# The first mixer's output product: eight half-size block products become seven

## Chip, cores and metric

The kernel runs on one core of one Trainium2 chip. The metric is the device time of one execution in microseconds (us). Before the change it is 1657.04 us, the median of 3 runs (1656.95 to 1657.22).

## The reference, cut to what matters

Two transformer blocks run one after the other on a sequence of 512 tokens with 1024 channels, all in float32. The first block has a mixer, a mixture of experts (top 2 of 32) and an embedding gate; the second has attention, a gated recurrence and a large MLP. What changes is the last product of the first mixer:

```
merged = sigmoid(gate_a) * (y_a @ w_up_a) + sigmoid(gate_b) * (y_b @ w_up_b)
x = x + merged @ w_out
h = rmsnorm(x, g_ffn)          # then the router and the experts read h
```

`merged` is 512 x 1024 and `w_out` is 1024 x 1024.

## The kernel before

TensorE multiplies in the reduced format float32r. To keep float32 accuracy every operand is split into a high part (a copy by ScalarE into float32r) and a low part (VectorE: value minus high), and each product is three matmul passes: high by high, high by low, low by high. `split_hi` (L1329) makes the high part of a weight chunk of 512 x 512, `split_lo` (L2246) the low part, `rest` (L2263) the low part of activations. `merged` lies in `ga_fm`, channels on partitions, in eight tiles of 128 channels by 512 tokens; its parts are `act_hi` and `act_lo`.

The output product before (L3742 to L3747 on TensorE): four chunks of `w_out`, each 512 channels in by 512 out. SyncE loads each into one of two buffers `w_stage` (`load_chunk`, L827) once the chunk two places ahead is split. `tile_passes` (L3445) multiplies one tile of 128 tokens by one chunk: 4 channel tiles x 3 passes = 12 matmuls of 128 x 128 by 512 columns. There are 4 chunks x 4 token tiles = 16 such groups, 192 matmuls. The first column half is summed in the PSUM banks `gb` and added to the rows `x` by VectorE (`add_tile`, L2598); in the second half the groups are paired by token tile (`paired_unit`, L3566), so that the row ends come early: each finished token tile is added, squared and scaled (`root` L1583, `scale_rows` L2268), transposed by TensorE (`turn_rows`, L3494) and multiplied by the router's weights. The transposes of rows 0 stand before the last group.

Ahead of it `g_upa` and `g_upb` (the two up-projections, 48 matmuls a unit) end in VectorE's gate and merge steps (L2557 and L2589, a pair for each of the eight tiles). VectorE's instructions follow a written order: merge pairs 0 to 3, `split_lo` of w_out's chunk 0, the low parts of merged tiles 0 to 3, merge pairs 4 to 7, `split_lo` of chunk 1, low parts of tiles 4 to 7, and then the additions. ScalarE (L1561 to L1575) alternates in the same way. SyncE's order is: weights of `g_upb`, the rows `x` again (L912), the four chunks of `w_out` (L913), the gain, the router's weights, and the experts' first weights into `ring[0]` to `ring[5]` (`load_half`, L931, 2 MB each). GpSimd issues nothing between the head sums of the mixer and the embedding gate. In the last MLP GpSimd issues transfers that add a block of weights in HBM to a block in SBUF (`add_block`, L1304).

Waits are on counting semaphores; an instruction whose wait is not met holds all that stand behind it on its engine. Here `w_stage`, `w_hi` and `w_lo` are 2 buffers each (L220 to L222).

Of the kernel before, what the change touches and what calls it, by code (L numbers as in the profile page):

```python
# [75 lines left out]
def two_blocks(nc, A, out):  # L76
# [37 lines left out]
    g_out = Gemm(g_upb, 2, 2, "dve")  # L114
# [30 lines left out]
    with ctx:  # L145
# [680 lines left out]
        def _(sp):  # L826
# [82 lines left out]
            load_units(g_upb, A["w_up_b"][0], 0)  # L909
# [3 lines left out]
            load_units(g_out, A["w_out"][0], 0)  # L913
            load_gain(1, A["g_ffn"][0])
# [20 lines left out]

            sp.dma_start(route_f[:, :, 0:NG], A["w_grp"][0].rearrange("(k p) n -> p k n", p=P))\
# [104 lines left out]
            for s in range(2):  # L1041
                sp.wait_ge(gates_stored[s], 16 * KT)
# [186 lines left out]


# [95 lines left out]
        def _(act):  # L1326
# [240 lines left out]
            for u in range(2):  # L1567
                split_hi(g_out.chunk0 + u, u)

                act.wait_ge(pe_tiles, 4 * (g_upa if u == 0 else g_upb).chunk1)  # L1570
                for k in range(4 * u, 4 * u + 4):
                    act.wait_ge(merged, k + 1)
# [2822 lines left out]
```

## Time and profile before

| | |
|---|---|
| median of the runs | 1657.04 us |
| the profiled execution | 1658.27 us, its span 1656.6 us |
| TensorE busy | 1642.8 us (99%), 10312 matmuls |
| VectorE, ScalarE, GpSimd busy | 1044.9, 718.4 and 123.2 us |
| granted TensorE clock | 0.999 |
| HBM traffic | 215 GB/s over the span |

The span runs from the first to the last instruction; the execution's own time also has what lies around it. A matmul's shown duration overlaps the next one's, so its price in a dense stream is the distance of starts. "us to landing" of a transfer counts from its issue.

### The profile page before, as it was taken

How to read it: one execution, taken by the hardware profiler on the slowest of the kernel's cores; microseconds unless marked ns; L12 is line 12 of the kernel's file. 1: busy time of each engine (PE TensorE's matmuls, PEld its weight loads, DVE VectorE, ACT ScalarE, POOL GpSimd, SP SyncE). 2: the span in 40 equal slices, each digit the busy share in tenths (PEclk: the TensorE clock that was granted, in tenths of full speed). 3: DMA queues.
4: the chain of work that ended last, by engine and by line, in shares of the span. 5: the costliest groups of instructions: out<-in, count | busy, mean ns of one | idle time of the engine just before them, and what ended most of it. 6: DMA issues, size and time to landing. Idle time of an engine off the chain costs nothing.

```text
span 1656.6 us, 25306 instructions
## 1 busy us (share of the span) xinstructions
PE 1642.8 (99%) x10312; PEld 1240.0 (75%) x10312; DVE 1044.9 (63%) x1373; ACT 718.4 (43%) x911; POOL 123.2 (7%) x175
## 2 busy tenths in 40 slices
PE   9999999999999999999999999999999999999998
PEld 7899998864545535554688877788888889889986
DVE  6989778453243334324578746567675577878887
ACT  6576553421101101111366533344643367757775
POOL 4000100000000000000111022210020000000000
PEclk9999999999999999999999999999999999999999
DMA  7132324888999999999551232124366527467864
GB/s 269 63 112 92 103 77 169 350 334 338 424 412 430 428 427 430 429 427 428 226 178 42 91 102 77 52 77 133 110 222 167 145 93 209 106 185 220 206 141 126
DMA packets 93697, 358.28 MB, mean 216 GB/s; under 512 B 8016, under 2 KB 8032, under 8 KB 81312
## 3 DMA queue, kind: packets, MB, share of 16 engines
q1 hardware_dynamic: 81264, 330.67, 52.0%
q0 software_dynamic: 12336, 26.23, 8.1%
q8 instruction: 71, 1.16, 0.3%
q14 instruction: 26, 0.21, 0.0%
HBM read 349.54 MB, written 7.34 MB: 215 GB/s over the span
## 4 chain that ended last, share of the span: by engine, by line
PE 96%; DVE 2%; DMA 1%; ACT 0%; issue 0%; POOL 0%; DVEq 0%; POOLq 0%; ACTq 0%
PE bank L3467 31%; PE bank L3896 13%; PE bank L4341 9%; PE bank L3630 9%; PE bank L4316 9%; PE bank L3909 7%; PE bank L3801 4%; PE bank L3842 3%; PE bank L4075 2%; PE bank L3492 2%; PE bank L3513 1%; DMA w_stage<-in_w_proj_gla 1%; PE bank L4105 1%; PE bank L4128 1%; PE bank L4175 1%
## 5 line engine op out<-in xcount | busy, mean ns | idle before, releaser
L3467 PE MATMUL bank<-act_hi,w_hi 128*128 128x512 f32 x544 | 215.5, 396 | 2.1 <-DVE gs_fm L2557 1.7
L3896 PE MATMUL bank<-ring,xgT 128*64 128x512 f32 x992 | 215.9, 592 | 0.6 <-ACT xgT L1641 0.6
L3467 PE MATMUL bank<-act_hi,w_lo 128*128 128x512 f32 x544 | 212.1, 390 | 0.0
L3467 PE MATMUL bank<-act_lo,w_hi 128*128 128x512 f32 x544 | 211.8, 389 | 0.0
L3896 PEld LDWEIGHTS bank<-ring,xgT 128*64 128x64 f32 x992 | 71.9, 137 | 140.2 <-issue 140.0
L1336 ACT ACTIVATE w_hi<-w_stage 128x2048 fp32r<-128x2048 f32 x50 | 95.9, 1919 | 138.9 <-PE bank L3467 128.7
L2249 DVE TENSOR_TENSOR w_lo<-w_stage,w_hi 128x2048 fp32r<-128x2048 f32 x50 | 115.2, 2303 | 62.9 <-ACT w_hi L1336 61.3
L4341 PE MATMUL bank<-down,part_hi 128*128 128x512 f32 x448 | 138.2, 390 | 0.1
L3467 PEld LDWEIGHTS bank<-act_hi,w_hi 128*128 128x128 f32 x544 | 102.1, 188 | 26.1 <-issue 2.8
L1671 ACT ACTIVATE y_hi_sb<-bank,slot_tables 128x512 fp32r<-128x512 f32 x32 | 22.0, 687 | 225.6 <-PE bank L3909 224.2
L3467 PEld LDWEIGHTS bank<-act_hi,w_lo 128*128 128x128 f32 x544 | 102.1, 188 | 21.8
L3467 PEld LDWEIGHTS bank<-act_lo,w_hi 128*128 128x128 f32 x544 | 102.2, 188 | 20.2
L3909 PE MATMUL bank<-ring,gatedT 128*64 128x512 f32 x512 | 113.4, 595 | 0.0
L2759 DVE TENSOR_TENSOR gated<-gated,bank 128x512 f32<-128x512 f32 x16 | 11.0, 688 | 161.3 <-PE bank L3896 161.3
L4341 PEld LDWEIGHTS bank<-down,part_hi 128*128 128x128 f32 x448 | 83.8, 188 | 18.2 <-issue 1.1
L3909 PEld LDWEIGHTS bank<-ring,gatedT 128*64 128x64 f32 x512 | 35.4, 137 | 69.5 <-issue 66.4
L4341 PE MATMUL bank<-down,part_lo 128*128 128x512 f32 x224 | 87.2, 389 | 0.0
L2731 DVE TENSOR_TENSOR x_tm<-x_tm,bank 128x512 f32<-128x512 f32 x128 | 78.6, 681 | 0.3 <-PE bank L3842 0.3
L2775 DVE SCALAR_TENSOR_TENSOR y_lo_sb<-bank,slot_tables,y_hi_sb 128x512 fp32r<-128x512 f32 x32 | 23.5, 751 | 69.9 <-ACT y_hi_sb L1671 69.6
L3630 PE MATMUL bank<-row_hi,slot_hi 128*128 128x256 f32 x224 | 63.5, 284 | 0.0
L4316 PE MATMUL bank<-act_lo,slot_hi 128*128 128x256 f32 x224 | 63.4, 283 | 0.0
L4316 PE MATMUL bank<-act_hi,slot_lo 128*128 128x256 f32 x224 | 63.4, 283 | 0.0
(600 smaller groups left out, 3782.8 us busy)
## 6 DMA issues: line engine op xcount, KB each, us to landing
ring<-in_w SPq DMA_DIRECT2D x93, 2048.0 KB, 14.5
w_stage<-in_w_in SPq DMA_DIRECT2D x39, 1024.0 KB, 5.2
w_stage<-in_w_ff SPq DMA_DIRECT2D x19, 1024.0 KB, 6.3
b_sum<-in_w_ff POOLq DMA_DIRECT2D x12, 1024.0 KB, 10.9
w_stage<-in_w_out SPq DMA_DIRECT2D x8, 1024.0 KB, 5.7
b_one<-in_w_ff SPq DMA_DIRECT2D x6, 1024.0 KB, 7.0
stage<-in_w_ff SPq DMA_DIRECT2D x5, 1024.0 KB, 5.6
x_tm<-in_x SPq DMA_DIRECT2D x8, 512.0 KB, 9.4
```

The source lines that it names most:

```text
L1336: act.activation(w_hi[s][:, 0:ktiles, :], w_stage[s][:, 0:ktiles, :], ACT.Copy)\
L2249: dve.tensor_tensor(w_lo[s][:, 0:ktiles, :], w_stage[s][:, 0:ktiles, :], w_hi[s][:, 0:ktiles, :].bitcast(F32), ALU.subtract).then_inc(w_lo ...
L2731: dve.tensor_tensor(xt, xt, bank[:, :], ALU.add).then_inc(moe_added, 1)
L3467: ins = pe.matmul(banks[j][:, :], left, right, start=(kc == 0 and k == 0 and n_pass == 0), stop=(kc == g.chunks - 1 and k == g.ktiles - 1 ...
L3492: return pe.transpose(dst, src, ident[0:rows, 0:rows])
L3630: ins = pe.matmul(bank_of[:, 256 * f:256 * f + 256], left[:, k, cols], right[:, k, :], start=(n in (0, 1, 3) and f == 0 and k == 0 and n_p ...
L3801: return pe.matmul(bank[:, (k % 2) * 2 * P:(k % 2 + 1) * 2 * P], part[:, t, k * P:(k + 1) * P], sel[:, t, :], start=start, stop=(part is x ...
L3842: ins = pe.matmul(bank[:, :], selT[:, t * P:(t + 1) * P], part[:, half], start=(part is y_hi_sb), stop=(part is y_lo_sb))
L3896: ins = pe.matmul(dst[mine, :], xgT[:, 4 * kh + k, slots], up_weights(2 * w + kh, q, k, ahead), start=(kh == 0 and k == 0), stop=(kh == 1 ...
L3909: return pe.matmul(gb[1 + nh][mine, :], gatedT[:, k, mine], ring[4 + k // 2][:, 4 * q + 2 * (k % 2) + nh, :], start=(k == 0), stop=(k == 3 ...
L4316: ins = pe.matmul(bank[:, 256 * f:256 * f + 256], left[:, k, cols], right[:, k, :], start=(n in (0, 1, 3) and f == 0 and k == 0 and n_pass ...
L4341: ins = pe.matmul(part_bank[h][n][j][:, :], left[:, ka, cols], right[:, k, :], start=(part_first[n] and kc == 0 and k == 0 and n_pass == 0 ...
```

## The change

`merged` is cut into token halves (near: tokens 0 to 255, far: 256 to 511) and channel halves, and `w_out` into four blocks of 512 x 512. Seven products of 256 tokens x 512 channels x 512 columns take the place of eight; each is 2 token tiles x 12 = 24 matmuls. They need sums of blocks. The weight sums T1 to T4 are made by negated copies on ScalarE (`out_negated`) and by five accumulating transfers that GpSimd issues (`out_block_added`): `o_t2` = W12 - W22 + W21, `o_t3` = W12 - W22, `o_t1` = W22 - W21, `o_t4` = W11 - T2, where W12 is rows 0 to 511, columns 512 to 1023. The four sums of activations are VectorE instructions (`out_sum`, 128 x 1024 each) in `ga_fm` and `o_s2`. Products that share a result follow each other in the same PSUM banks: VectorE adds the bank to the one place, and TensorE then goes on summing in it for the next, so products 2, 3, 5 and 6 wait for the addition of the product they continue (`out_bank`, `out_first`). SyncE loads four blocks itself: three blocks of `w_out` directly for use or as start of a sum (W11 and W21 in `w_stage`, W22 in `o_t3`) and W12 in `o_b22`. The experts' first weights move: ring 5 and 4 ahead, 0, 3, 1 and 2 during and after the products. The semaphore counts of `gates_stored`, which is used again, are raised. The core of the diff:

```diff
-    g_out = Gemm(g_upb, 2, 2, "dve")
+    g_out = Gemm(g_upb, 1, PARTS + 1, "dve", tiles=2 * PARTS)
...
+        o_t1 = at("o_t1", F + 0, [P, 4, 512])
+        o_b22 = at("o_b22", F + 16, [P, 4, 512])
+        o_t2, o_t3, o_t4 = (at(f"o_t{n}", F + page, [P, 4, 512]) for n, page in ((2, 4), (3, 20), (4, 12)))
+        o_s2 = at("o_s2", F + 48, [P, 4, 256])
+        o_t2_hi, o_t2_lo = at("o_t2_hi", F + 8, [P, 4, 512], F32R), at("o_t2_lo", F + 4, [P, 4, 512], F32R)
+        o_t4_hi, o_t4_lo = at("o_t4_hi", F + 8, [P, 4, 512], F32R), at("o_t4_lo", F + 12, [P, 4, 512], F32R)
+        o_b22_hi, o_b22_lo = at("o_b22_hi", F + 20, [P, 4, 512], F32R), at("o_b22_lo", F + 16, [P, 4, 512], F32R)
...
+        out_bank = (mb[0:2], mb[2:4], mb[2:4], mb[2:4], gb[2:4], mb[2:4], gb[2:4])
+        out_first = (True, True, False, False, True, False, False)
...
+        OUT_PLACES = ((2, 0), (2, 0), (2, 1), (0, 1), (0, 1), (0, 0), (2, 1))
+        O_SUM_2, O_SUM_4, O_SUM_3, O_SUM_1 = 32, 48, 16, 32
+        OUT_ADDS = (3, 2)
+        OH_LESS_12, OH_LESS_12_AGAIN, OH_LESS_11, OH_T2, OH_LESS_T2, OH_S2, OH_S3, OH_S1, OH_S4 = range(KT + 1, KT + 10)
+        O_S1, O_S2, O_S3, O_S4 = range(KT + 1, KT + 5)
+        OL_T2, OL_S2, OL_S3, OL_S1, OL_S4 = range(KT + 1, KT + 6)
...
-            load_units(g_upb, A["w_up_b"][0], 0)
+            load_unit(g_upb, 0, A["w_up_b"][0], 0)
+            sp.wait_ge(o_gated, NH)
+            sp.dma_start(o_t3[:, :, :], out_block(1, 1)).then_inc(out_far, 16)
...
-            load_units(g_out, A["w_out"][0], 0)
-            load_gain(1, A["g_ffn"][0])
+            for i in range(2):
+                load_chunk(g_out.chunk0 + i, i, A["w_out"][0], slice(0, 512), i)
+            sp.wait_ge(merged_high, OH_LESS_12)
+            sp.dma_start(o_b22[:, :, :], out_block(0, 1)).then_inc(out_far, 16)
...
+            sp.wait_ge(out_far, 32)
...
-            sp.wait_ge(y_lo, AT_MERGED + KT)
-            for m in range(2):
-                load_half(m, 0)
-            sp.wait_ge(w_lo_done, split_count(g_out.chunk1 - 1))
+            sp.wait_ge(y_lo, 2 * NH)
+            load_half(5, 0)
+            sp.wait_ge(merged, KT)
+            load_half(4, 0)
+            sp.wait_ge(w_lo_done, split_count(out_chunk(1)))
+            for i in range(2):
...
+            sp.wait_ge(w_lo_done, split_count(out_chunk(4)))
+            sp.wait_ge(pe_tiles, out_product(2))
+            load_half(0, 0)
+            sp.wait_ge(merged_sums, O_S4)
+            load_gain(1, A["g_ffn"][0])
...
+            sp.wait_ge(merged_low, OL_S4)
+            load_half(3, 0)
+            sp.wait_ge(pe_tiles, out_product(5))
+            load_half(1, 0)
+            sp.wait_ge(pe_tiles, 4 * g_out.chunk1)
+            load_half(2, 0)
...
+            def out_block_added(dst, i, q, n):
+                pool.dma_start(dst[:, :, :], out_block(i, q), accum_op=ALU.add).then_inc(out_block_added_in[n], 16)
+            pool.wait_ge(merged_high, OH_LESS_12)
+            out_block_added(o_t2, 0, 1, 0)
+            pool.wait_ge(merged_high, OH_LESS_12_AGAIN)
+            out_block_added(o_t3, 0, 1, 1)
+            pool.wait_ge(out_block_added_in[0], O_SUM_2 - 16)
+            out_block_added(o_t2, 1, 0, 0)
+            pool.wait_ge(merged_high, OH_LESS_11)
+            pool.wait_ge(out_block_added_in[1], O_SUM_3)
+            out_block_added(o_t1, 1, 1, 1)
+            pool.wait_ge(merged_high, OH_LESS_T2)
+            out_block_added(o_t4, 0, 0, 0)
...
+            def out_negated(dst, src):
+                act.activation(dst[:, :, :], src[:, :, :], ACT.Copy, scale=-1.0).then_inc(merged_high, 1)
+            act.wait_ge(out_far, 16)
+            out_negated(o_t2, o_t3)
             split_hi(g_upb.chunk0, 0)
+            act.wait_ge(merged_high, OH_LESS_12)
+            out_negated(o_t3, o_t3)
             for h in range(NH):
...
+            act.wait_ge(w_loaded[1], ((g_out.chunk0 + 1) // 2 + 1) * 16)
+            out_negated(o_t1, w_stage[1])
+            split_hi(out_chunk(0), 0)
+            act.wait_ge(pe_tiles, 4 * g_upa.chunk1)
+            for k in range(4):
+                act.wait_ge(merged, k + 1)
+                act.activation(act_hi[:, k, :], ga_fm[:, k, :], ACT.Copy).then_inc(y_hi, 1)
+            act.wait_ge(out_block_added_in[0], O_SUM_2)
+            act.activation(o_t2_hi[:, :, :], o_t2[:, :, :], ACT.Copy).then_inc(merged_high, 1)
+            out_negated(o_t4, o_t2)
+            split_hi(out_chunk(1), 1)
+            act.wait_ge(pe_tiles, 4 * g_upb.chunk1)
+            act.wait_ge(merged, KT)
...
+            act.wait_ge(pe_tiles, out_product(0))
+            act.wait_ge(merged_sums, O_S2)
+            act.activation(act_hi[:, near_k, far_t], o_s2[:, :, :], ACT.Copy).then_inc(merged_high, 1)
+            act.wait_ge(out_block_added_in[1], O_SUM_3)
+            act.activation(w_hi[0][:, :, :], o_t3[:, :, :], ACT.Copy).then_inc(w_hi_done, 1)
+            act.wait_ge(merged_sums, O_S3)
+            act.activation(act_hi[:, far_k, near_t], ga_fm[:, far_k, near_t], ACT.Copy).then_inc(merged_high, 1)
+            act.wait_ge(pe_tiles, out_product(1))
+            act.wait_ge(out_block_added_in[1], O_SUM_1)
+            act.activation(w_hi[1][:, :, :], o_t1[:, :, :], ACT.Copy).then_inc(w_hi_done, 1)
+            act.activation(act_hi[:, far_k, far_t], ga_fm[:, near_k, near_t], ACT.Copy).then_inc(merged_high, 1)
+            act.wait_ge(pe_tiles, out_product(2))
+            act.wait_ge(out_block_added_in[0], O_SUM_4)
+            act.activation(o_t4_hi[:, :, :], o_t4[:, :, :], ACT.Copy).then_inc(w_hi_done, 1)
+            act.wait_ge(w_lo_done, split_count(out_chunk(3)))
+            act.wait_ge(out_far, 32)
+            act.activation(o_b22_hi[:, :, :], o_b22[:, :, :], ACT.Copy).then_inc(w_hi_done, 3)
...
-            act.wait_ge(w_lo_done, split_count(g_out.chunk1 - 1))
-            for t in range(NT):
-                act.wait_ge(out_dve, g_out.tile0 + 4 + t + 1)
-                if t == 3:
-                    own.settle()
-                own.did(half_square(0, t, ssq))
+            for t in (2, 3):
+                act.wait_ge(out_dve, out_added(1, t - 2))
+                own.did(half_square(first_half(t), t, ssq))
+            act.wait_ge(early_in, EARLY_IN)
+            act.activation(early_p_hi[:, :, :], early_p[:, :, :], ACT.Copy).then_inc(p_hi, 1)
+            act.activation(early_ple_hi[:, :, :], early_ple[:, :, :], ACT.Copy).then_inc(p_hi, 1)
+            act.wait_ge(pe_tiles, out_product(4))
+            act.wait_ge(merged_sums, O_S4)
+            act.activation(act_hi[:, far_k, far_t], ga_fm[:, near_k, far_t], ACT.Copy).then_inc(merged_high, 1)
+            own.settle()
+            for t in (0, 1):
+                act.wait_ge(out_dve, out_added(4, t))
+                own.did(half_square(first_half(t), t, ssq))
             own.settle()
...
+            dve.wait_ge(merged, KT)
+            out_sum(m22, m21, m22, ALU.add)
+            split_lo(out_chunk(1), 1)
+            dve.wait_ge(y_hi, AT_MERGED + KT)
+            rest(act_lo[:, far_k, far_t], m11, act_hi[:, far_k, far_t]).then_inc(y_lo, 4)
+            dve.wait_ge(merged_sums, O_S1)
+            out_sum(o_s2[:, :, :], m22, m11, ALU.subtract)
+            dve.wait_ge(merged_high, OH_LESS_T2)
+            rest(o_t2_lo[:, :, :], o_t2[:, :, :], o_t2_hi[:, :, :]).then_inc(merged_low, 1)
+            dve.wait_ge(rows_again, 16 + 16 * NT)
+            out_low(near_k, far_t, o_s2[:, :, :], OH_S2)
+            out_add(0, 0)
+            out_add(0, 1)
+            out_sum(m21, m11, m21, ALU.subtract)
+            out_add(1, 0)
+            out_weights_low(3, w_lo[0], o_t3, w_hi[0])
+            out_add(1, 1)
+            out_low(far_k, near_t, m21, OH_S3)
+            out_add(2, 0)
+            out_low(far_k, far_t, m22, OH_S1)
+            out_add(2, 1)
+            out_weights_low(4, w_lo[1], o_t1, w_hi[1])
+            out_add(3, 0)
+            out_add(3, 1)
+            out_sum(m12, m12, o_s2[:, :, :], ALU.subtract)
+            out_weights_low(5, o_t4_lo, o_t4, o_t4_hi)
+            out_add(4, 0)
+            out_add(4, 1)
+            out_weights_low(6, o_b22_lo, o_b22, o_b22_hi, parts=3)
+            out_low(far_k, far_t, m12, OH_S4)
+            out_add(5, 0)
+            out_add(5, 1)
             def add_tile(u, j, width=512):
                 xt = x[:, j, u * 512:(u + 1) * 512]
                 return dve.tensor_tensor(xt, xt, gb[j][:, :], ALU.add)
...
-            merged_half = half_split(AT_MERGED)
-            for kc in range(2):
-                for j in range(4):
-                    merged_half(kc, j)
-                    tile_passes(g_out, g_out.chunk0 + kc, g_out.tile0 + j, kc, kc, j, fm=False)
-            paired_unit(g_out, 1, {7: lambda: turn_rows(1, 0)})
+            def out_passes(n, j):
+                k0, t0 = ((0, 256), (4, 256), (0, 256), (4, 0), (4, 256), (0, 0), (4, 256))[n]
+                hi, lo = ((w_hi[0], w_lo[0]), (w_hi[1], w_lo[1]), (o_t2_hi, o_t2_lo), (w_hi[0], w_lo[0]),
+                          (w_hi[1], w_lo[1]), (o_t4_hi, o_t4_lo), (o_b22_hi, o_b22_lo))[n]
+                cols = slice(t0 + j * P, t0 + (j + 1) * P)
+                for k in range(4):
+                    for n_pass, (left, right) in enumerate(((act_hi, hi), (act_hi, lo), (act_lo, hi))):
+                        ins = pe.matmul(out_bank[n][j][:, :], left[:, k0 + k, cols], right[:, k, :],
+                                        start=(out_first[n] and k == 0 and n_pass == 0),
+                                        stop=(k == 3 and n_pass == 2), skip_group_check=True)
+                ins.then_inc(pe_tiles, 6 if (n, j) == (PARTS - 1, 1) else 2)
+            def out_operands(n):
+                if n in out_split:
+                    pe.wait_ge(w_lo_done, split_count(out_chunk(n)))
+                if n < 2:
+                    pe.wait_ge(y_lo, AT_MERGED + 4 * n + 4)
+                elif n != 5:
+                    pe.wait_ge(merged_low, {2: OL_S2, 3: OL_S3, 4: OL_S1, 6: OL_S4}[n])
+            for n in range(PARTS):
+                out_operands(n)
+                for j in range(2):
+                    if n in (2, 3, 5, 6):
+                        pe.wait_ge(out_dve, out_added({2: 1, 3: 2, 5: 3, 6: 4}[n], j))
+                    out_passes(n, j)
+                    if (n, j) == (PARTS - 1, 0):
+                        turn_rows(1, 0)
```

## Rows read from the trace of the kernel before

**Rows 1.** The page, busy time of each engine and its share of the span.

```profile
PE 1642.8 (99%) x10312; PEld 1240.0 (75%) x10312; DVE 1044.9 (63%) x1373; ACT 718.4 (43%) x911; POOL 123.2 (7%) x175
```

**Rows 2.** The chain that ended last, 281 to 347 us: start, us, what, how many.

```profile
281.75 41.03 PE bank L3467 x181
...
330.41 1.02 PE bank L3492 x8
...
346.66 7.09 PE bank L3896 x32
```

**Rows 3.** Timeline of VectorE: start, duration, operation and shape, waits in brackets.

```profile
273.14 2.29 DVE L2249 TENSOR_TENSOR w_lo<-w_stage,w_hi 128x2048 fp32r<-128x2048 f32 x1 [0.60 <-ACT w_hi L1336]
275.35 2.49 DVE L2264 TENSOR_TENSOR act_lo<-ga_fm,act_hi 128x512 fp32r<-128x512 f32 x4
277.76 0.68 DVE L2557 TENSOR_TENSOR gb_fm<-gb_fm,bank 128x512 f32<-128x512 f32 x1
...
280.41 0.68 DVE L2557 TENSOR_TENSOR gb_fm<-gb_fm,bank 128x512 f32<-128x512 f32 x1
...
317.41 1.23 DVE L2264 TENSOR_TENSOR early_p_lo<-early_p,early_p_hi 128x1024 fp32r<-128x1024 f32 x1 [2.07 <-ACT early_p_hi L1613]
```

**Rows 4.** Timeline of ScalarE, 244 to 276 us.

```profile
244.09 1.90 ACT L1336 ACTIVATE w_hi<-w_stage 128x2048 fp32r<-128x2048 f32 x1
...
271.19 1.92 ACT L1336 ACTIVATE w_hi<-w_stage 128x2048 fp32r<-128x2048 f32 x1 [8.96 <-PE bank L3467]
273.02 2.17 ACT L1573 ACTIVATE act_hi<-ga_fm 128x512 fp32r<-128x512 f32 x4
```

**Rows 5.** Timeline of SyncE's queue, 248 to 265 us: the issues.

```profile
248.34 0.37 SPq L835 DMA_DIRECT2D w_stage<-in_w_up_b  x1
248.75 2.17 SPq L912 DMA_DIRECT2D x_tm<-in_x  x4
...
255.47 0.40 SPq L835 DMA_DIRECT2D w_stage<-in_w_out  x1
...
264.72 0.39 SPq L835 DMA_DIRECT2D w_stage<-in_w_out  x1
```

**Rows 6.** Issues of 264 to 265 us, KB and us to landing.

```profile
w_stage<-in_w_out SPq DMA_DIRECT2D x1, 1024.0 KB, 5.0
```

**Rows 7.** Windows, 250 to 261 us: length, busy time by engine, PEclk, DMA share, GB/s.

```profile
250.00:261.00 11.00, 11.00 (x50) 9.06 (x50) 10.19 (x15) 3.11 (x5) 0.00 (x0) 1.00 0.97 376
```

**Rows 8.** Accumulating transfers alone: issues at 1591 and 1595 us, and their landings.

```profile
1591.12 1.28 POOL L1307 DMA_DIRECT2D w_stage<-in_w_ff  x1 [36.94 <-ACT w_stage L1966]
1594.85 1.28 POOL L1307 DMA_DIRECT2D w_stage<-in_w_ff  x1 [2.45 <-ACT w_stage L1966]
...
w_stage<-in_w_ff POOLq DMA_DIRECT2D x1, 1024.0 KB, 8.6
...
w_stage<-in_w_ff POOLq DMA_DIRECT2D x1, 1024.0 KB, 10.8
```

**Rows 9.** An accumulating and a plain transfer issued together at 1258 us, and their landings.

```profile
1258.16 1.41 POOL L1307 DMA_DIRECT2D b_sum<-in_w_ff  x1 [39.36 <-ACT b_sum L1966]
...
b_sum<-in_w_ff POOLq DMA_DIRECT2D x1, 1024.0 KB, 11.2
w_stage<-in_w_out SPq DMA_DIRECT2D x1, 1024.0 KB, 5.7
```

**Rows 10.** A plain transfer issued behind two accumulating ones, at 1527.84 us; timeline and landing.

```profile
1524.95 2.60 POOL L1307 DMA_DIRECT2D b_sum<-in_w_ff  x2 [8.70 <-DMA b_sum<-in_w_ff]
...
w_stage<-in_w_ff SPq DMA_DIRECT2D x1, 1024.0 KB, 14.8
```

**Rows 11.** Windows in the experts, 700 to 750 us; columns as in rows 7.

```profile
700.00:750.00 50.00, 50.00 (x262) 25.38 (x260) 17.42 (x40) 4.96 (x8) 0.00 (x0) 1.00 1.01 429
```

**Rows 12.** Timeline of TensorE at the kernel's start, the first matmuls after it was idle.

```profile
6.38 2.04 PE L3513 MATMUL bank<-w_hi,raw_hi 128*128 128x512 f32 x4
8.23 1.35 PE L3513 MATMUL bank<-w_lo,raw_hi 128*128 128x512 f32 x4
```

More of the change, by code:

```diff
@@ L531, in two_blocks @@
         counters, COUNTERS = att_masked, NT + 3
+        out_far, merged_sums, merged_high, merged_low = route_in, merged, x_hi, x_lo
+        out_block_added_in = gates_stored
         early_stored = (wsp_masked, ln_sd)
@@ L625, in loaded, with block_in @@
         def loaded(h, buffers, k):
-            base, per = {"one": (1, ONE_LOADS), "sum": (2, SUM_LOADS), "added": (KT, ADDS)}[buffers]
+            base, per = {"one": (1, ONE_LOADS), "sum": (2, SUM_LOADS)}[buffers]
             return 16 * (base + per * h + k)
+        def block_in(n, h, k):
+            return 16 * (OUT_ADDS[n] + KT + ADDS * h + k)
         def weight_block(h, i, q, kc):
@@ L947, in _ @@
                 .then_inc(early_in, 16)
-            for m in range(2, 6):
-                load_half(m, 0)
-            sp.wait_ge(pe_tiles, 4 * g_out.chunk1)
+            sp.wait_ge(w_lo_done, split_count(out_chunk(4)))
[3 more added lines that the diff above has]
+            load_gain(1, A["g_ffn"][0])
+            sp.wait_ge(pe_tiles, out_product(4))
             for q in range(2):
@@ L1566, in _ @@
             split_hi(g_upb.chunk0 + 1, 1)
[L1567 to L1572, printed above, removed]
-                    act.activation(act_hi[:, k, :], ga_fm[:, k, :], ACT.Copy).then_inc(y_hi, 1)
-            split_hi(g_out.chunk0 + 2, 0)
-            split_hi(g_out.chunk0 + 3, 1)
-            def half_square(u, t, sums):
-                half = slice(u * 512, (u + 1) * 512)
+            act.wait_ge(w_loaded[1], ((g_out.chunk0 + 1) // 2 + 1) * 16)
@@ L1580, in half_square @@
+            act.wait_ge(out_block_added_in[0], O_SUM_4)
[3 more added lines that the diff above has]
+            act.activation(o_b22_hi[:, :, :], o_b22[:, :, :], ACT.Copy).then_inc(w_hi_done, 3)
+            def half_square(half, t, sums):
                 return act.activation(squared[t % 3][:, :], x[:, t, half], ACT.Square, scale=float(D) ** -0.5,
@@ L1583, in root @@
             def root(t):
-                act.wait_ge(out_dve, g_out.tile0 + 4 + NT + t + 1)
-                own.did(half_square(1, t, half_ms))
+                act.wait_ge(out_dve, out_added(5, t) if t < 2 else out_added(6, t - 2))
+                own.did(half_square(second_half(t), t, half_ms))
                 own.settle()
@@ new lines, in _, with out_sum, out_low, out_weights_low @@
+            m22, m12 = ga_fm[:, near_k, near_t], ga_fm[:, near_k, far_t]
+            m21, m11 = ga_fm[:, far_k, near_t], ga_fm[:, far_k, far_t]
+            def out_sum(dst, left, right, op):
+                dve.tensor_tensor(dst, left, right, op).then_inc(merged_sums, 1)
+            def out_low(k, t, src, high):
+                dve.wait_ge(merged_high, high)
+                rest(act_lo[:, k, t], src, act_hi[:, k, t]).then_inc(merged_low, 1)
+            def out_weights_low(n, lo, raw, hi, parts=1):
+                dve.wait_ge(w_hi_done, split_count(out_chunk(n)))
+                rest(lo[:, :, :], raw[:, :, :], hi[:, :, :]).then_inc(w_lo_done, parts)
@@ L3758, in logits_of @@
                 return ins
-            pe.wait_ge(route_in, 32)
+            pe.wait_ge(route_in, 64)
             for t in range(1, NT):
```

67 lines of the change are left out of this document (41 added, 26 removed).

## The prediction, made before the changed kernel ran

> **What bounds the kernel now.** I read the busy times of the page first: TensorE is busy 99% of the span [rows 1], so any matmul taken away from it can count. The chain that ended last is next: from 281.75 us it is 181 matmuls of the output product in 41.03 us, 0.2267 us each, then, after transposes and the last group, the transposes and router products to 333.4 us, of which the last row's transpose starts at 330.41 [rows 2]. So TensorE sets the pace here and waits for nobody. Then I read the timelines of the engines that feed it, since the change makes their queues longer: VectorE [rows 3], ScalarE [rows 4], SyncE [rows 5], and the landings of both kinds of transfer [rows 6 to 10].
>
> **The saving.** 192 matmuls become 168; all are 128 x 128 by 512 columns in the same three-pass order. 24 x 0.2267 = 5.44 us go, all on the chain. One product lasts 5.44 us, a token tile 2.72. Without any wait product 0 would run from 281.8 to 287.3. The additions in the banks, the sums and the splits replace it on other engines; what matters is when they end.
>
> **The transfers.** The first megabytes decide. A plain block of 1 MB lands in 5.0 us alone [rows 6]; where the engines are full they move 376 GB/s at 0.97 [rows 7], 388, so the block takes 2.7 us of all of them and 2.3 besides. An accumulating block lands in 8.6 us alone, and one issued 3.73 us after it lands at 1605.65, 5.9 after the first [rows 8]: it costs 6.0 us of all engines. The two kinds add up: issued beside a plain block, an accumulating one lands in 11.2 [rows 9], and 8.6 + 2.7 = 11.3. ScalarE's copy of 244.09 ends at 246.0 [rows 4], the first negation (1.9) at 247.9, and GpSimd issues the first addition into `o_t2` there, the one into `o_t3` about 4 us later, and the second into `o_t2` when the first has landed. SyncE issues the weights of `g_upb` at 248.34, the rows `x` (2 MB) from 248.75, W11 at 255.47 and W21 at 264.72 [rows 5], W12 right behind. Until `o_t2` is whole that is 3 x 6.0 + 6 x 2.7 = 34.2 us of engine time from about 249.4, the engines never idle: data to 283.6, landed at 284.6. W21 stands behind 4 MB on its queue; with even shares between the two queues its 5 x 2.7 = 13.5 us take 27, to 276.4, landed at 277.6 instead of the 269.7 of before. W22 into `o_t3` is issued earlier and I take it as landed when wanted. The shares are the least known term: in rows 9 the plain block had most of the engines (5.7 us, 0.7 above alone), in rows 10 it had little (14.8 us behind two accumulating ones). If the plain side always went first, W21 would land at 270.4, but the experts' ring 5 (2 MB, 5.4 us, issued when W12 has landed) would also go ahead of `o_t2`: 290. If the accumulating side went first, W21 would be last, at about 282. I take even shares, between the two.
>
> The Trainium skill says (DMA: Bandwidth & Descriptors, Queues, rings and completion order) that each transfer engine takes turns between its queues, a packet at a time. By that rule the shares are nearer to even than in either of my ends, which would leave the sum below; rows 9 and 10 show both a larger and a smaller share, so here the trace does not settle it.
>
> **ScalarE and VectorE up to product 1.** ScalarE negates W21 into `o_t1` ahead of the high part of W11: 277.6, 279.5, 281.4; the four copies of merged tiles take 2.17 [rows 4], to 283.5 (before: from 271.19, to 275.2). VectorE stands at the low part of W11 until 281.4, then 2.2, then four low parts 2.49 [rows 3]: 286.2. Product 0 starts at 286.3, a wait of 4.5, and ends at 291.7. VectorE comes to the last four merge pairs only now; two pairs take 280.41 - 277.76 = 2.65 [rows 3], four 5.3: `merged` complete at 291.5. ScalarE meanwhile: `o_t2` landed 284.6, high part 286.5, negation into `o_t4` 288.3, high part of W21 290.2, then waits for `merged`, copy of 128 x 1024 about 1.1 (half of 2.17) to 292.6. A VectorE step of 128 x 1024 is 1.23, its start-to-start about 1.15, one of 128 x 2048 2.29 and 2.2 [rows 3]. After 291.5: the sum S1 1.15, low part of W21 2.2, low part of the tiles 1.15: 296.0. Product 1 starts at 296.1: a wait of 4.4. Together 8.9 us against 287.3 (to 0.1).
>
> **From product 1 on.** VectorE next: S2 1.15, low part of T2 2.2, low part of S2 1.15, two bank additions 1.3 (0.68 each, rows 3), S3 1.15, addition of product 1's first tile 0.7: 7.7 us, to 303.7, while product 1 ends at 301.5. Product 2 sums on in that bank, so TensorE waits 2.2. Its second tile waits 0.1 more, for a low part of 2.2 between the two additions. Products 2 to 5 take 21.8 us and VectorE has four low parts of weights, four of 128 x 1024 and eight additions beside them, 4 x 2.2 + 4 x 1.15 + 8 x 0.66 = 18.7: no further wait. ScalarE has some 12 us there and the transfers into `o_t1` and `o_t4` (6.0 each, done by about 300 and 304) are wanted at about 303.5 and 309: hidden; if both came 3 us late they would cost what they are late. After product 5 VectorE has the last addition 0.7, the low part of p 1.2 and the scaling of row 0, 0.2 + 1.3: 3.4 us plus hand-overs, and TensorE wants row 0 after 2.7: 0.8. Token tiles 2 and 3 follow as before, with VectorE 1 us later against TensorE's end; of that 1 us the last transpose can lose between nothing and all, I take 0.3. Negations on ScalarE before 260 move `w_hi` of `g_upb` by under 0.1; their cover is TensorE's own work until 260.
>
> **Nothing else moves.** GpSimd's waits hold nobody: its next work is the embedding gate, after the experts. SyncE's new waits stand ahead of the router's weights and the early ring halves, and the gated heads for which it waits ahead of `g_upb`'s second block are done before that block was issued anyway, 248.34 [rows 5]. In the experts TensorE and the transfer engines are both full, 50.00 of 50 us and 1.01 [rows 11], and TensorE doesn't wait. The last four ring loads are 8 MB after about 319 us, 20 us at 429 GB/s, to 340; the first expert product stood at 346.66 [rows 2] and moves to about 353: 13 us of cover. Should that cover go, the cost is its lateness.
>
> **Sum.** -5.4 + 8.9 + 2.2 + 0.1 + 0.8 + 0.3 = +6.9. The profiled execution took 1658.27 (span 1656.6), 1.23 above the median 1657.04; the sum is a difference inside that span, to 1665.2 for such an execution, and 1663.9 for the median. A measurement of this kernel tells 0.2%, 3.3 us, from no change.
>
> **Rivals.** *Even or mixed shares, as above*: with W21 in time and `o_t2` whole at 284.6, ScalarE has W21's high part at 290.2 and VectorE ends 3.4 us later, 293.6, in place of 296.0, so +4.5 at the least; at the most +8.5, with `o_t2` whole at about 288.5: 1661.5 to 1665.5; for it speaks that the transfer time adds up in rows 8 and 9. Chance 0.52.
>
> *The additions don't queue* (W21 by 271.7, `o_t2` by 281, so the transfers overlap better than rows 8 and 9 say): the W21 negation still puts ScalarE 2.4 us behind 271.19. Product 1 then waits for `merged`, S1 and two low parts until 290.2, 2.9; +2.9 + 2.2 + 0.1 + 0.8 + 0.3 - 5.4 = +0.9: 1657.9. For it: the plain block of rows 9, hardly slowed. Against: 34.2 us of work in 32. Chance 0.19.
>
> *Faster*: the only way is that VectorE isn't late. If W21 lands by 270 and VectorE's merge pairs keep their times, product 1 starts by 288.4 and product 2 follows with a wait under 1: -5.4 + 1.1 + 0.8 + 0.3 = -3.2 or better, at best 1652.7 with half of the tail's waits gone. It decides at a landing of W21 at 270; against it stand the 3 us of steps that VectorE has between `merged` and product 1. Chance 0.05.
>
> *One side goes first*: `o_t2` at 290 gives product 1 a start at 299, +9.5, 1666.5; W21 at 282 gives +11, 1668. For it: rows 9 and 10, each in its direction. Chance 0.14.
>
> *A cold TensorE*: no stretch of the trace that I read shows a granted clock below 1.00, so no row prices it; the first four matmuls after the idle start took 8.23 - 6.38 = 1.85 us instead of 0.91 [rows 12], which product 2's wait of 2.2 would absorb. If all of product 1 ran at half speed, 5.4 us more less 2.2 is +3.2: 1666.9. Chance 0.10.
>
> The Trainium skill (TensorE: Matmul & The Clock Gate, Part 1: The HAM clock gate) says that an idle array falls from 2.4 to 1.2 GHz. With two waits of over 4 us that rule would make this last rival's time out of mine.
>
> **How the numbers follow.** Faster by over 0.2%: 0.05. Within 0.2%: the second rival, 0.19. Slower: the other three, 0.76. The range goes from just under the second rival to the later shares, 1656.8 to 1668.5; it leaves out the faster case and the tail of the late ones. Inside the likeliest case it is 1661.5 to 1665.5.
>
> **What would show it.** In the changed profile: 168 matmuls of the product at 0.227; a TensorE wait ahead of product 0 or 1 of 7 to 10 us in all, released by VectorE's low parts; a wait of about 2 ahead of product 2 behind an addition to `x`; ScalarE idle until W21 lands (277) and until `o_t2` is whole (285); DMA share near 1 from 249 to 284. I am wrong if the accumulating transfers take under 5 us of the engines each, or if ScalarE finds both landed when it comes to them; and if the experts' TensorE starts to wait for rings.

## The result, and the profile after

The changed kernel takes 1666.91 us (median of 6 runs, 1666.54 to 1667.41), the kernel before beside it 1657.05 (6 runs, 1656.46 to 1657.29): +9.9 us, a ratio of 1.0059 with a 95% interval of 1.0048 to 1.0069. That is slower, inside the range of 1656.8 to 1668.5, 3.0 above the forecast of 1663.9. The profiled execution took 1666.54, with a span of 1664.9.

TensorE has 24 matmuls less than in [rows 1] and 2.5 us less busy time, though 24 matmuls are 5.44 us. From the page, busy times:

```profile
PE 1640.3 (99%) x10288; PEld 1236.5 (74%) x10288; DVE 1061.9 (64%) x1387; ACT 733.2 (44%) x919; POOL 128.9 (8%) x180
```

The chain that ended last answers to [rows 2]. There it was one piece of TensorE's from 281.75 to the first transpose at 322.78; now it runs through ScalarE and VectorE from `g_upb`'s end to product 2 (start us, duration, what):

```profile
282.85 1.90 ACT w_hi L1419
...
284.77 2.29 DVE w_lo L2366
287.06 2.41 DVE act_lo L2381 x4
...
298.14 1.22 DVE act_lo L2381
...
306.08 0.69 DVE x_tm L2736
...
306.91 22.08 PE bank L3914 x96
...
332.28 1.09 PE bank L3655 x8
```

All of this trace up to here is 0.4 us earlier than before's: `g_upb` ends at 281.35. From there to the first transpose it is 50.93 us, 9.9 more than the 41.03 of [rows 2]; 0.3 more comes before the router's first reduction. The experts after it are only shifted: their first product stood at 346.66 [rows 2] and stands at 356.42. The two profiled spans differ by 8.3 us and not by 9.8, because the execution profiled before lost 1.7 us in one wait of TensorE for VectorE's `gs_fm`, at 1243 us, where the other lost 0.3. So the question is where 15.6 us went between 281.35 and 332.28 beside the matmuls' own 35.4. TensorE's timeline gives the starts of products 0, 1 and 2, with the wait before each in brackets:

```profile
289.62 0.77 PE L3914 MATMUL bank<-w_hi,act_hi 128*128 128x512 f32 x1 [8.11 <-DVE act_lo L2381]
...
299.50 0.47 PE L3914 MATMUL bank<-w_hi,act_hi 128*128 128x512 f32 x1 [1.95 <-DVE act_lo L2381]
...
306.91 0.47 PE L3914 MATMUL bank<-o_t_hi,act_hi 128*128 128x512 f32 x1 [1.68 <-DVE x_tm L2736]
```

The waits are 8.1, 1.95, 1.7, and 0.6 ahead of the first transpose, 12.4 in all. The other 3 us lie inside the products: product 0 runs from 289.62 to 297.55, 7.9 in place of 5.4, and product 1, and products 2 to 5 together, are each 0.3 longer than their matmuls at 0.2267. The windows say why the first one is (length, busy time of PE, PEld, DVE, ACT and POOL, PEclk, DMA share, GB/s):

```profile
285.00:287.00 2.00, 0.00 (x0) 0.00 (x0) 2.00 (x2) 2.00 (x5) 0.00 (x0) 0.50 0.99 63
293.00:294.00 1.00, 1.00 (x3) 0.74 (x3) 1.00 (x2) 0.00 (x0) 0.00 (x0) 0.50 1.07 459
...
295.00:297.00 2.00, 2.00 (x11) 1.65 (x10) 2.00 (x2) 0.94 (x1) 0.00 (x0) 1.00 0.97 361
```

While TensorE was idle its granted clock fell to 0.50, the 1.2 GHz level, and matmuls then started 0.427 us apart until about 294.3, 0.2267 after that.

What holds VectorE is ScalarE, and what holds ScalarE is a transfer. ScalarE's timeline (L1646 is a negation, L1419 the high part of a weight chunk), to be laid beside [rows 4], where the high part of W11 stood at 271.19:

```profile
281.03 1.91 ACT L1646 ACTIVATE o_t<-w_stage 128x2048 f32<-128x2048 f32 x1 [19.27 <-DMA w_stage<-in_w_out]
282.85 1.89 ACT L1419 ACTIVATE w_hi<-w_stage 128x2048 fp32r<-128x2048 f32 x1
284.65 2.17 ACT L1663 ACTIVATE act_hi<-ga_fm 128x512 fp32r<-128x512 f32 x4
286.73 1.89 ACT L1665 ACTIVATE o_t_hi<-o_t 128x2048 fp32r<-128x2048 f32 x1
```

ScalarE is idle for 19.3 us until W21 has landed, at 281.0. W11 landed at 272.9 (issued 254.87, 18.0 us) and lay there. The high part of `o_t2` waits for nothing when its turn comes. The issues of 263.5 to 265 us, W21, the second addition into `o_t2` and W12 (KB, us to landing), against 5.0 for W21 in [rows 6]:

```profile
w_stage<-in_w_out SPq DMA_DIRECT2D x1, 1024.0 KB, 16.9
o_t<-in_w_out POOLq DMA_DIRECT2D x1, 1024.0 KB, 16.7
o_b<-in_w_out SPq DMA_DIRECT2D x1, 1024.0 KB, 19.0
```

The queues of that stretch, 272 to 278 us (packets, MB, share of the engines' time; q0 is GpSimd's with the additions, q1 SyncE's):

```profile
q0 software_dynamic: 385, 0.79, 70.6%
q1 hardware_dynamic: 384, 0.78, 39.1%
```

The packets, one row of 2 KB each, are as many on one side as on the other. The time is not: 71% to 39%.

### The profile page after: what moved, and what is told of

Read it like the earlier page. It is cut to its first block, busy times and chain, and to the rows that moved or that the text cites. A ratio compares the mean times of both kernels' runs of the same rounds, so it can differ in the third digit from the quotient of the medians.

```text
span 1664.9 us, 25288 instructions
## 1 busy us (share of the span) xinstructions
PE 1640.3 (99%) x10288; PEld 1236.5 (74%) x10288; DVE 1061.9 (64%) x1387; ACT 733.2 (44%) x919; POOL 128.9 (8%) x180
## 4 chain that ended last, share of the span: by engine, by line
PE 94%; DVE 4%; issue 1%; ACT 1%; POOL 0%; DVEq 0%; POOLq 0%; ACTq 0%
PE bank L3630 29%; PE bank L4084 13%; PE bank L4529 9%; PE bank L3793 8%; PE bank L4504 8%; PE bank L4097 7%; PE bank L3989 4%; PE bank L4030 3%; PE bank L4263 2%; PE bank L3655 2%; PE bank L3914 1%; PE bank L3676 1%; PE bank L4293 1%; PE bank L4316 1%; PE bank L4363 1%
## 5 line engine op out<-in xcount | busy, mean ns | idle before, releaser
L2366 DVE TENSOR_TENSOR w_lo<-w_stage,w_hi 128x2048 fp32r<-128x2048 f32 x48 | 110.5, 2303 | 65.4 <-ACT w_hi L1419 63.7
L1419 ACT ACTIVATE w_hi<-w_stage 128x2048 fp32r<-128x2048 f32 x48 | 92.1, 1919 | 103.9 <-PE bank L3630 95.3
L4097 PEld LDWEIGHTS bank<-ring,gatedT 128*64 128x64 f32 x512 | 35.4, 137 | 69.5 <-issue 66.4
```

Of the source, the lines that this page charges most:

```text
L1419: act.activation(w_hi[s][:, 0:ktiles, :], w_stage[s][:, 0:ktiles, :], ACT.Copy)\
L2366: dve.tensor_tensor(w_lo[s][:, 0:ktiles, :], w_stage[s][:, 0:ktiles, :], w_hi[s][:, 0:ktiles, :].bitcast(F32), ALU.subtract).then_inc(w_lo ...
L4097: return pe.matmul(gb[1 + nh][mine, :], gatedT[:, k, mine], ring[4 + k // 2][:, 4 * q + 2 * (k % 2) + nh, :], start=(k == 0), stop=(k == 3 ...
```

## The experiments

Times are medians, ratios are to the kernel before on the same chip (1657.02, 1656.71 and 1656.84 us in the three groups of runs).

### e1_neg_late: W21's negation behind W11's steps

```
-act.wait_ge(w_loaded[1], ...); out_negated(o_t1, w_stage[1])
 split_hi(out_chunk(0), 0)
 ... act_hi of merged tiles 0 to 3
+act.wait_ge(w_loaded[1], ...); out_negated(o_t1, w_stage[1])
 ... o_t2_hi, out_negated(o_t4, o_t2), split_hi(out_chunk(1), 1)
```

> ScalarE's negation of W21 moves from ahead of W11's high part to behind the four copies of merged tiles; nothing is added or taken away. Theory A (W21's late landing, 281.0 us in the changed kernel's trace, holds ScalarE and with it W11's high part): W11 has landed at 272.9, its low part and those of the tiles are ready at about 279.5, product 0 starts with g_upb's end at 281.4 without a wait, product 1 at about 292 (negation to 283, the two steps on o_t2 to 286.7, W21's high part 288.6, its low part 290.8, the tiles' 292); product 2 waits about 2. The time falls by about 7 us to 1660. Theory B (the idle array's low clock is what costs): also no idle stretch of 8 us ahead of product 0, the clock stays, but the gain is only the 2.2 us that product 0 lasted longer: 1664.7. Theory C (VectorE's steps alone are too many, whatever lands when): no change, 1666.9.

Measured: 1659.76 us, ratio 1.0018 (1.0008 to 1.0027), 7.2 under the changed kernel. ScalarE's timeline and TensorE's waits:

```profile
272.27 1.92 ACT L1419 ACTIVATE w_hi<-w_stage 128x2048 fp32r<-128x2048 f32 x1 [11.03 <-DMA w_stage<-in_w_out]
...
280.56 1.92 ACT L1646 ACTIVATE o_t<-w_stage 128x2048 f32<-128x2048 f32 x1 [4.30 <-DMA w_stage<-in_w_out]
```

```profile
PE bank L3914 <- DVE act_lo L2381: 5.1, 1, 5.1
```

W21 landed as late as before (280.6), and product 0 didn't wait. The wait of 8.1 was one instruction in ScalarE's queue: theory A, to 0.3 us. Theories B and C fall. Product 1 waited 5.1, the clock fell again (0.50 from 291 to 295 us), and product 1 took 8.0 us. That used up the wait of product 2 and some 0.6 us more: the addition that product 2 waits for ended at 298.74, 0.14 goes by for the hand-over (306.77 to 306.91 in the chain above), and product 2 started at 299.49.

### e2_rows_late: the rows x behind w_out on SyncE's queue

```
-for t in range(NT): sp.dma_start(x[:, t, :], x_dram[t])
 ... W11, W21, W12 (o_b22)
+for t in range(NT): sp.dma_start(x[:, t, :], x_dram[t])
```

> The rows x (2 MB, issued ahead of W11 and W21 in the changed kernel) go out behind W11, W21 and W12. Theory A (queueing of transfers makes W21 late): W11 lands at about 262, W21 at about 272 in place of 281.0, o_t2 stays whole at about 281; product 0 starts at 281.4 without a wait, product 1 at about 290.6 (last merge pairs 286.1, sum, two low parts), product 2 waits 2: about 1658.4. Theory A' (W21's lateness comes from the accumulating transfers alone, and what is ahead on its own queue doesn't matter): W21 still lands near 280, 1665 to 1667. Theory C (VectorE alone): 1666.9.

Measured: 1661.37 us, ratio 1.0026 (1.0016 to 1.0036), 5.5 under the changed kernel and 3 above theory A's figure. The landing of W21, and TensorE's two waits:

```profile
w_stage<-in_w_out SPq DMA_DIRECT2D x1, 1024.0 KB, 11.1
```

```profile
283.32 0.73 PE L3914 MATMUL bank<-w_hi,act_hi 128*128 128x512 f32 x1 [2.36 <-DVE act_lo L2381]
...
293.21 0.47 PE L3914 MATMUL bank<-w_hi,act_hi 128*128 128x512 f32 x1 [2.60 <-DVE act_lo L2381]
```

W21 landed at 274.7, not 272, and `o_t2` was whole at 274.2, not 281, 6.6 us sooner than in the changed kernel. Of the 2.7 us by which W21 missed, 2.4 came through ScalarE to product 0. The queues from 254 to 258 us show most of the reason, this run's first and then the changed kernel's:

```profile
q0 software_dynamic: 413, 0.82, 112.1%
q1 hardware_dynamic: 1, 0.00, 0.2%
```

```profile
q0 software_dynamic: 211, 0.43, 58.1%
q1 hardware_dynamic: 207, 0.73, 49.4%
```

With the rows gone, the plain queue had nothing to move until W11's first packets at 258, although W11 was issued at 254.4, and the additions had the engines alone. From 258 to 264 both sides moved 2 KB packets, as many on one as on the other, and W11 landed at 266.4, not 262. So what stands ahead of W21 counts (A' falls); my reckoning of the rates was off, which the run with half rows below takes up.

### e3_no_add: the additions cut to 8 KB

```
-pool.dma_start(dst[:, :, :], out_block(i, q), accum_op=ALU.add)
+pool.dma_start(dst[:, 0:1, 0:16], out_block(i, q)[:, 0:1, 0:16], accum_op=ALU.add)
```

> The five accumulating transfers move 8 KB each (16 columns of one row group) in place of 1 MB: the weight sums are left out but for that corner, every wait stays. Theory A (W21 and o_t2 are late because the accumulating transfers take engine time): W21 lands at about 270, o_t2 is there when ScalarE comes to it; product 0 doesn't wait, product 1 waits 1 to 2 us for VectorE (last merge pair 284, sum 285.2, two low parts 288.5 against 286.8), product 2 about 2, the tail 0.8: 1656.5, with 1655 to 1658 as bounds. Theory C (VectorE's added steps cost the time whatever lands when): above 1662. My prediction's second rival priced this case at 1657.9.

Measured: 1655.15 us, ratio 0.9987 (0.9978 to 0.9997). W21 landed 5.1 us after its issue, at 269.4. TensorE's waits from 281 to 330 us (total, times, longest):

```profile
PE bank L3915 <- DVE x_tm L2737: 1.7, 1, 1.7
PE bank L3915 <- DVE act_lo L2382: 0.8, 1, 0.8
PE bank L3656 <- DVE xn L2395: 0.6, 1, 0.6
```

-5.4 + 0.8 + 1.7 + 0.6 = -2.3 us, measured -1.9. The transfers that the change adds are what cost 11.8 us; the longer queues of ScalarE and VectorE cost 3.1 of the 5.4 saved.

### e4_warm and e4b_warm: TensorE kept busy ahead of product 0

```
+for _ in range(140):        # e4b_warm: 36
+    pe.matmul(mb[0][:, 0:P], ident[:, :], ident[:, :], start=True, stop=True, ...)
 for n in range(PARTS): out_operands(n) ...
```

> 140 products of the 128 x 128 identity into a bank that product 0 then overwrites fill TensorE's idle 8.2 us ahead of product 0 (7.9 us at 0.0567 each), so the array doesn't idle and product 0 runs at 0.2267 us a matmul in place of 0.427. Theory A (product 1 is set by VectorE, so the low clock in product 0 is absorbed): product 0 ends at about 295.1, product 1 starts at 299.4 as before after a wait of about 4.1, time within 0.5 of 1666.9. Theory B (the low clock costs what product 0 is longer): 1664.7.

Measured: 1683.51 us, ratio 1.0159 (1.0142 to 1.0176). It tells nothing of the two theories, only that my filler was mispriced: the identity products are float32, not float32r. TensorE's timeline, with two records for each of the 140, and product 0 behind them:

```profile
281.95 31.42 PE L3907 MATMUL bank<-ident 128*128 128x128 f32 x280
313.13 0.48 PE L3917 MATMUL bank<-w_hi,act_hi 128*128 128x512 f32 x1
```

(313.13 - 281.95) / 140 = 0.223 us each at 128 columns, against 0.2267 for a float32r pass of 512. They ran on for some 23 us past the moment at which product 0 could have started. The next expectation has 30.3 us and 0.217, from a view that ended at 312 and held 135 of them. With 36:

> 36 identity products in place of 140, since the run before showed them at 0.217 us each (30.3 us for 140), not 0.057: 36 fill 7.8 of the 8.2 idle us ahead of product 0. Theory A (product 1 is set by VectorE, so the low clock in product 0 is absorbed): product 0 starts at 289.6, lasts 5.4 us in place of 7.6, product 1 starts at 299.4 as before, time within 0.5 of 1666.9. Theory B (the low clock costs what product 0 is longer): 1664.7.

Measured: 1667.59 us, ratio 1.0061 (1.0045 to 1.0078), 0.7 above the changed kernel where theory A had allowed 0.5. TensorE's timeline, the filler, product 0 and product 1:

```profile
281.54 8.20 PE L3907 MATMUL bank<-ident 128*128 128x128 f32 x72
289.86 0.47 PE L3917 MATMUL bank<-w_hi,act_hi 128*128 128x512 f32 x1
...
299.76 0.76 PE L3917 MATMUL bank<-w_hi,act_hi 128*128 128x512 f32 x1 [4.20 <-DVE act_lo L2381]
```

Product 0 now ran at the full clock from the start and was done at 295.4. Product 1 started no earlier than before (299.76 to 299.50), since VectorE had not come further. The wait ahead of it grew from 1.95 to 4.2, the clock fell there (0.51 from 300 to 305), and product 1 took up the slow matmuls. Product 2 started at 307.71, some 0.6 us after VectorE's addition would have let it. Nothing was gained; B would have been 2.2 us faster. So in the changed kernel the low clock in product 0 costs nothing, because VectorE sets the start of product 1; where it falls into product 1, here and in e1_neg_late, it costs some 0.6.

### e6_both_late: both moves together

> The moves of e1_neg_late and e2_rows_late together. Theory A (ScalarE's queue behind a late W21, and the rows ahead of W21 on its queue, are the whole loss above e3_no_add): W21 lands at 274.7 and o_t2 is whole before 276 as in e2_rows_late, ScalarE has W21's high part when g_upb frees its buffer, 281.8 to 283.7; product 0 doesn't wait, product 1 waits 0.8, product 2 1.7, as in e3_no_add, and the clock never falls: 1655.3. Theory D (the five accumulating transfers also cost later, by contention or late weights for products 3 to 5): above 1657.

Measured: 1655.05 us, ratio 0.9988 (0.9978 to 0.9998); once more as e10_both_late_again:

> e6_both_late once more, beside e8_dve_order on one chip, so that the two can be told apart: 1655.0, under the kernel before by 0.1%.

1654.61 us, ratio 0.9986 (0.9977 to 0.9995). TensorE's waits between 281 and 330 us:

```profile
PE bank L3914 <- DVE x_tm L2736: 1.7, 1, 1.7
PE bank L3914 <- DVE act_lo L2381: 0.8, 1, 0.8
PE bank L3655 <- DVE xn L2394: 0.6, 1, 0.6
```

They are those of e3_no_add to the tenth, with all five additions in place, and the granted clock stays at 1.00. Theory A holds, D falls: two moved steps take back all that the transfers had cost, 11.9 us.

### e5_order, e7_no_add_dve and e8_dve_order: the order of the engines' steps

The cut of VectorE's diff:

```
-out_sum(m22, m21, m22, ALU.add)                      # S1
 split_lo(out_chunk(1), 1); rest(act_lo[far_k, far_t] ...)
+out_sum(m22, m21, m22, ALU.add)
 ... S2, o_t2_lo, low part of S2
-out_add(0, 0); out_add(0, 1)
-out_sum(m21, m11, m21, ALU.subtract)                 # S3
-out_add(1, 0); out_weights_low(3, ...); out_add(1, 1)
+out_add(1, 0); out_add(1, 1)
+out_sum(m21, m11, m21, ALU.subtract)
+out_weights_low(3, ...)
 ... product 2's additions, low parts of S3, S1 and o_t1
+out_add(0, 0); out_add(0, 1)
 ...
+rest(early_p_lo ...)                                 # from behind out_add(5, 1)
 out_add(5, 0); out_add(5, 1)
```

> e6_both_late with ScalarE's steps ordered by need (negation, W21's high part, far tiles' high part, then the two steps on o_t2) and VectorE's too: low part of W21 and of the far tiles ahead of sum S1, product 1's bank additions ahead of product 0's and of S3, the low part of p ahead of product 5's additions. If VectorE's order sets the remaining waits: product 1 waits 0.3 in place of 0.8, product 2 0.6 in place of 1.7, product 3 up to 0.4, row 0's turn 0 in place of 0.6: 1653.5, 3.5 under the kernel before. If they come from its load and not its order: 1655, as e6_both_late.

Measured: 1656.17 us, ratio 0.9990 (0.9981 to 1.0000), not better than e6_both_late. Its waits:

```profile
PE bank L3914 <- DVE o_t_lo L2381: 1.8, 1, 1.8
PE bank L3655 <- DVE xn L2394: 0.8, 1, 0.8
PE bank L3914 <- DVE x_tm L2736: 0.6, 1, 0.6
PE bank L3914 <- DVE act_lo L2381: 0.3, 1, 0.3
```

The waits ahead of products 1 and 2 became the 0.3 and 0.6 expected, but product 5 waits 1.8 for the low part of `o_t4`. I had moved the two steps on `o_t2` back on ScalarE, and with them the negation into `o_t4` on which GpSimd's last addition waits: issued at 287.54 it took 19.1 us beside the ring loads, where in e6_both_late, issued at 281.02, it took 13.1. The ring's packets are large: from 294 to 296 us of e5_order each queue moved 39 packets, 0.08 MB of the addition and 0.62 MB of the ring. A step that looked late enough for its reader was late for a transfer that starts from it.

> e3_no_add (the accumulating transfers cut to 8 KB, so the weight sums are left out but for a corner) with VectorE's order of e5_order and ScalarE's of the changed kernel. The floor for the order of VectorE without contention: 1653.3 to 1654; if e5_order stands above it by more than 0.5, what is left there is the transfers.

Measured: 1653.65 us, ratio 0.9978 (0.9968 to 0.9988).

> e6_both_late with VectorE's order of e5_order and ScalarE's order of e6_both_late (o_t2's high part and negation ahead of W21's high part). In e5_order the addition into o_t4 was issued only at 287.2 and landed at 306.9, since its negation had moved back, and product 5 waited 1.8 us for it. If that was all that e5_order lost, product 5 doesn't wait here: waits of 0.3, 0.6 and 0.5 to 0.8 are left, 1653.8, and the run stands 1.2 under e6_both_late. If the order of VectorE brings nothing by itself: 1655, as e6_both_late.

Measured: 1653.10 us, ratio 0.9977 (0.9968 to 0.9986): 3.7 us under the kernel before, 1.5 under e10_both_late_again beside it, 13.8 under the changed kernel. What is left of TensorE's waits there:

```profile
PE bank L3914 <- DVE x_tm L2736: 0.6, 1, 0.6
PE bank L3655 <- DVE xn L2394: 0.5, 1, 0.5
PE bank L3914 <- DVE act_lo L2381: 0.3, 1, 0.3
```

-5.4 + 1.4 = -4.0, measured -3.7. With or without the additions the time is the same to 0.6 us. This version beats both kernels.

### e9_rows_2k: the same bytes in twice the packets

```
-sp.dma_start(x[:, t, :], x_dram[t])
+for q in range(2):
+    sp.dma_start(x[:, t, q * 512:(q + 1) * 512], x_dram[t][:, q * 512:(q + 1) * 512])
```

> The changed kernel with each transfer of 128 rows of x (4 KB a row) as two of half rows, 2 KB each: the same bytes ahead of W11 on the queue, twice the packets. Theory P (the transfer engines take a packet of either queue in turn, whatever its size, some 51 to 64 a us of each kind in the changed kernel's trace while both queues are full): x takes up to 6 us longer beside the additions, W11 lands at about 279 in place of 272.9, o_t2 is whole earlier, at about 277 in place of 280.8. Theory T (the queues share the engines' time, as I reckoned): W11 stays within 1.5 of 272.9. The time of the kernel hangs on W21, which comes after both: near 1667 either way.

Measured: 1668.05 us in one run. The landings of W11 (issued 254.91) and of the second addition into `o_t2` (issued 262.61):

```profile
w_stage<-in_w_out SPq DMA_DIRECT2D x1, 1024.0 KB, 23.5
```

```profile
o_t<-in_w_out POOLq DMA_DIRECT2D x1, 1024.0 KB, 15.6
```

W11 landed at 278.4, 5.5 later, and `o_t2` was whole at 278.2, 2.6 earlier. The queues from 256 to 262 us, where the rows go by:

```profile
q0 software_dynamic: 410, 0.81, 72.5%
q1 hardware_dynamic: 409, 0.74, 37.9%
```

The same window of the changed kernel:

```profile
q0 software_dynamic: 314, 0.64, 57.6%
q1 hardware_dynamic: 309, 1.13, 50.6%
```

But for the count that VectorE's wait asks for, nothing but the size of the rows' packets differs, and W11 was issued at the same time (254.87). Theory P holds, T falls: while both queues have packets to move, the turns go by packets.

## Why the prediction was right, and where it was off

- **The direction and the mechanism** are as forecast. The saving was 5.44 us; TensorE waited ahead of products 0 and 1 for VectorE's low parts, and VectorE for ScalarE, ScalarE for W21. e1_neg_late and e3_no_add show both links: moving one instruction in ScalarE's queue gave 7.2 us, taking the additions away 11.8.
- **The work of the transfers** was right. 34.2 us of engine time from 249.4 were to end in data at 283.6, landed at 284.6; the last of them, W12, landed at 264.54 + 19.0 = 283.5, 1.1 sooner. The share of the engines was 1.04 to 1.09 from 249 to 281, near 1 as forecast.
- **The order in which the work is done** is the step that failed: "even shares between the two queues", W21 at 277.6. It was at 281.0, and 3.4 us late. I shared the engines' time evenly, so that the plain side would have moved half of 388 GB/s. What is shared evenly is the packets (e9_rows_2k, and 385 to 384 in the window above). With 2 KB packets on both sides the plain queue moved 0.78 MB in 6 us, 131 GB/s, while an addition's packet kept an engine for 0.176 us (16 engines x 6 us x 0.706 / 385 packets) against 0.098 for a plain one. By [rows 8] and [rows 7] the ratio could have been had (6.0 to 2.7 us a MB); I used it for the sum, not for the turns. With turns by packet, the additions' 96 packets an engine are through before the plain side's 128 up to the end of W21, so that W21's data end with all the work but W12's: 249.4 + 34.2 - 2.7 = 280.9, an estimate from my own figures. In the trace `o_t2` was whole at 280.8, 3.8 sooner than forecast, and waited for by nobody.
- **The starts of the products.** I had 286.3, 296.1 and 303.7; on the clock of before they were 290.0, 299.9 and 307.3, which is 3.7, 3.8 and 3.6 later. The 3.4 us of W21 went through nearly unchanged, and they are more than the 3.0 us between forecast and result; the small terms below gave some back. How the two first waits divide (8.1 and 1.95, not 4.5 and 4.4) follows from the later start, and from product 0 lasting 2.5 us longer in front of the same VectorE.
- **The small terms.** Product 2 waited 1.7, not 2.2 + 0.1; the first transpose 0.6, not 0.8; the last transpose 0, and 0.3 was lost elsewhere on the way to the router.
- **The cold TensorE** came, where I had given it a chance of 0.10 and a price of 3.2 us. The clock fell in the wait ahead of product 0. By e4b_warm the price is nothing: VectorE sets product 1's start, also on the chain above. That this rival's figure, 1666.9, is the measured time is chance.
- **The rival in which one side goes first** had W21 last at about 282 and 1668. In time that is nearly what happened, by another cause: nobody went first; the packets took turns. The measured time is above the 1661.5 to 1665.5 of the case that I held likeliest (0.52); only the outer bound, taken from this rival (0.14), took it in.
- **The rival in which the additions don't queue** was priced at 1657.9. e3_no_add, without the additions, comes nearest to it: 1655.15. It was 2.8 too dear, since W21 then lands at 269.4, not at my 271.7; so VectorE had W11's low part at 273.2, finished its merge pairs 1.7 us after `g_upb`, and product 1 waited 0.8, not 2.9. The landing that I named for the faster case, 270, was so met, but it gave -1.9 and not -3.2: product 2's wait of 1.7 stayed, which VectorE's order made (0.6 with the other order in e7_no_add_dve and e8_dve_order).
- **The signs.** The waits ahead of products 0 and 1 were 10.05 us, at the edge of "7 to 10". ScalarE did not wait for `o_t2`, as I had expected at 285. An accumulating block took 5.6 us of the engines (32 packets of 0.176), above the 5 that would have proved me wrong.
- **Slips in the working**, none of which moves the forecast. The faster case at its best leaves out the whole tail of 1.1; with half of it gone it is 1653.3, not 1652.7. The cold rival's 3.2 on 1663.9 is 1667.1, not 1666.9. A start of product 1 at 299 is +9.8, not +9.5, and W21 at 282 is +11.3, not +11.

The Trainium skill (DMA: Bandwidth & Descriptors, Queues, rings and completion order) says that each transfer engine takes turns between its queues, packet by packet. The trace agrees, with 385 packets to 384 as the profile counts them, one row each, and e9_rows_2k shows it by packet size. I had put this rule beside my even shares as if it meant the same; with turns by packet, the estimate above puts W21's data at 280.9.

The Trainium skill (TensorE: Matmul & The Clock Gate, Part 1: The HAM clock gate) says that an idle array falls to 1.2 GHz. The trace agrees: TensorE was idle from 281.5 to 289.6 us, the granted clock was 0.50 from 285 to 294, and matmuls started 0.427 us apart.

## What to carry to other kernels

When accumulating and plain transfers run at once, count packets, not bytes: while both have packets to move, each side gets as many as the other, an addition's packet holds an engine nearly twice as long (0.176 us to 0.098 here), and what stands ahead of an urgent block on its own queue (here 2 MB of rows that nobody reads before 302) is paid for in turns. Ask of each new step on an engine with a written order what it waits for and who stands behind it; here a negation whose sum is read 24 us later stood ahead of the copy wanted next, and moving it and the rows turned +9.9 us into -2. In moving a step back, look also at the transfer that starts from it.

## What the runs showed of the hardware

- Turns by packet hold for very small packets too. From 290 to 291 us the changed kernel loads the router's weights, in rows of 16 and 128 bytes, beside an addition: 98 packets on each queue, but 0.20 and 0.01 MB.

```profile
q0 software_dynamic: 98, 0.20, 107.8%
q1 hardware_dynamic: 98, 0.01, 16.5%
```

- The clock fell after TensorE's waits of 8.1 (changed kernel), 5.1 (e1_neg_late), 4.2 (e4b_warm) and also after the two of 2.4 and 2.6 us (e2_rows_late, 0.59 from 283 to 285 and 0.65 from 293 to 295). It stayed at 1.00 through the waits of 1.95 and 1.7 in the changed kernel, and of 1.7 and 0.8 in e3_no_add and e6_both_late. Products that ran into it lasted 7.3 to 8.0 us in place of 5.4.
- A float32 product of 128 columns took 0.223 us, nearly as long as a float32r pass of 512 columns (0.2267).
- The share of the transfer engines reads above 1 where both queues work: 1.25 from 284 to 288 us in e6_both_late, at 209 GB/s. It shows that both are busy, not how much is moved.
